# A decoder trunk on one core: the differential mixer's softmax weights transposed by DMA instead of TensorE

## What is computed

```python
def _diff_attention(q1, q2, k1, k2, v, lam):
    ...
        p1 = _masked_softmax(jnp.einsum('bhqd,bhkd->bhqk', q1b, k1).astype(jnp.float32) * scale, mask)
        p2 = _masked_softmax(jnp.einsum('bhqd,bhkd->bhqk', q2b, k2).astype(jnp.float32) * scale, mask)
        p = p1 - lam * p2
        return jnp.einsum('bhqk,bhkd->bhqd', p.astype(v.dtype), v)
```

## Time and profile before

| what | value |
|---|---|
| median of 3 runs | 825.76 us (825.39 to 825.9) |
| profiled execution, its own time | 824.97 us |
| its span, first to last instruction | 823.2 us |
| PE busy | 815.3 us (99%) |
| DVE, ACT, POOL busy | 572.3, 474.9, 291.0 us |
| 16 DMA engines, queue 1 | 68.5% |

### The profile page before, as it was taken

How to read it: one execution, slowest core, us unless ns; L and a number is a source line. 1 busy time by engine, 2 the same in 40 slices (tenths; PEclk the granted TensorE clock), 3 DMA queues, 4 the chain that set the end, 5 groups by cost and what they waited for, 6 DMA issues and landing times.

```text
span 823.2 us, 10986 instructions
## 1 busy us (share of the span) xinstructions
PE 815.3 (99%) x4012; PEld 669.8 (81%) x4012; DVE 572.3 (70%) x837; ACT 474.9 (58%) x709; POOL 291.0 (35%) x301
## 2 busy tenths in 40 slices
PE   9999999999999999999999999999999999999998
PEld 6888878888888888888888888888788888888886
DVE  5696888868765666655456878898697666666542
ACT  6877654794465555443457775557944645545441
POOL 0078874405202433320000789563070043323100
PEclk9999999999999999999999999999999999999999
DMA  9866867784558777775566656767745687777751
GB/s 331 304 149 208 248 180 207 187 252 142 198 185 234 218 208 214 219 221 187 167 203 224 168 205 207 229 192 201 235 154 182 211 215 213 228 227 209 215 185 71
DMA packets 125765, 169.40 MB, mean 206 GB/s; under 512 B 62864, under 2 KB 65168, under 8 KB 125456
## 3 DMA queue, kind: packets, MB, share of 16 engines
q1 hardware_dynamic: 125424, 168.43, 68.5%
q10 hardware_dynamic: 288, 0.27, 0.1%
HBM read 153.47 MB, written 1.05 MB: 188 GB/s over the span
## 4 chain that ended last, share of the span: by engine, by line
PE 90%; POOL 4%; issue 2%; DVE 2%; ACT 1%; DMA 1%; SPq 0%; POOLq 0%; DVEq 0%; ACTq 0%
PE acc L726 83%; POOL p_halves L1549 1%; PE att L869 1%; POOL proj L1482 1%; PE att L805 1%; PE att L773 1%; PE att L860 1%; DMA w_raw<-in_w_in 1%; PE att L798 1%; PE acc L805 1%; POOL proj L1478 0%; DVE za L1327 0%; PE att L843 0%; ACT za L1075 0%; DVE eb L1321 0%
## 5 line engine op out<-in xcount | busy, mean ns | idle before, releaser
L1198 DVE TENSOR_TENSOR w_lo<-w_raw,w_hi 128x1024 fp32r<-128x1024 f32 (+1 forms) x276 | 367.2, 1344 | 147.1 <-ACT w_hi L968 144.6
L726 PE MATMUL acc<-w_hi,xt 128*128 128x512 f32 (+1 forms) x1728 | 431.2, 391 | 0.3 <-ACT xt L991 0.3
L968 ACT ACTIVATE w_hi<-w_raw 128x1024 fp32r<-128x1024 f32 (+1 forms) x275 | 286.2, 1051 | 163.9 <-PE acc L726 153.2
L726 PEld LDWEIGHTS acc<-w_hi,xt 128*128 128x128 f32 x1728 | 319.8, 188 | 65.2 <-issue 1.1
L726 PE MATMUL acc<-w_lo,xt 128*128 128x512 f32 (+1 forms) x864 | 230.0, 388 | 1.6 <-DVE w_lo L1198 1.6
L726 PEld LDWEIGHTS acc<-w_lo,xt 128*128 128x128 f32 x864 | 161.8, 188 | 34.9 <-DVE w_lo L1198 2.2
L1601 POOL COPY hid_t<-hid_halves_t 128x512 uint16<-128x512 uint16 x44 | 35.0, 823 | 95.9 <-DMA hid_halves_t<-hid_halves 81.5
L1592 POOL COPY hid_halves<-hid 128x512 uint16<-128x512 uint16 x44 | 45.6, 1065 | 64.3 <-DVE hid L1277 64.3
L1549 POOL COPY p_halves<-eb 128x768 uint16<-128x768 uint16 x24 | 30.0, 1279 | 97.4 <-DVE eb L1333 60.5
L1462 POOL TENSOR_SCALAR small<-small 128x2 f32<-128x2 f32 (+3 forms) x12 | 9.4, 786 | 152.2 <-ACT sq_dump L1066 133.9
L1609 POOL TENSOR_TENSOR merged<-merged,prod 128x1024 f32<-128x1024 f32 x10 | 32.5, 3254 | 58.0 <-DVE prod L1249 57.1
(11 more groups left out here) (175 smaller groups left out, 715.0 us busy)
## 6 DMA issues: line engine op xcount, KB each, us to landing
w_raw<-in_w_ffn SPq DMA_DIRECT2D x88, 512.0 KB, 4.2
w_raw<-in_w_gate SPq DMA_DIRECT2D x64, 512.0 KB, 4.1
w_raw<-in_w_ffn_down SPq DMA_DIRECT2D x44, 512.0 KB, 4.0
w_raw<-in_w_in SPq DMA_DIRECT2D x39, 512.0 KB, 5.1
w_raw<-in_w_branch SPq DMA_DIRECT2D x16, 512.0 KB, 4.5
w_raw<-in_w_out SPq DMA_DIRECT2D x16, 512.0 KB, 3.3
bg<-in_b_gate SPq DMA_DIRECT2D x8, 512.0 KB, 5.4
w_raw<-in_w_in SPq DMA_DIRECT2D x8, 396.0 KB, 4.3
```

The costliest lines, as they stand in the source:

```text
L726: return pe.matmul(acc[bank0 + t][:, 0:N], x_part[:, k0 + k, t * P:(t + 1) * P], w_part[:, k, 0:N], start=first, stop=last)
L968: act.activation(w_hi[:, n % WR, :, 0:N], w_raw[:, n % RAW, :, 0:N], copy).then_inc(s_hi, 1)
L1198: dve.tensor_tensor(w_lo[:, n % WR, :, 0:N], w_raw[:, n % RAW, :, 0:N], w_hi[:, n % WR, :, 0:N].bitcast(F32), ALU.subtract).then_inc(s_lo, 1)
```

## The change

For B, the eight rows `pt` are taken out of the plan. Heads 0 and 1 are now dealt, transposed and joined together (`pdeal` and `pjoin` of ("B", 0)), heads 2 and 3 as ("B", 1), through one pair of planes of their own, `p_halves_b` and `p_halves_t_b`. Heads 0 and 1 are multiplied with V in turn 30, heads 2 and 3 in turn 38. `o` moves from turn 38 to 39, `deal` D from 31 to 33, `join` D from 35 to 36, SP's transpose for `join` D from its turn 40 to 41. The reduction for `prep` C no longer waits for POOL's `prep` B but for ACT's `brs`, which reads the same small tile. `cks` uses bank `S0` instead of `TP`, and `cs` uses `OB` instead of `S0`.

```diff
-TURNS = [("A", 0), ("A", 1), ("C", 0), ("C", 1), ("D", 0), ("D", 1), ("D", 2), ("D", 3)]
-TURN_P = (21, 22, 43, 47, 52, 53, 55, 56)
-TURN_AT = {33: "C", 40: "D"} | {CHUNKS.index(("ffn", j, 3)) + 9: j for j in range(N_FFN)}
+TURNS = [("A", 0), ("A", 1), ("B", 0), ("B", 1), ("C", 0), ("C", 1), ("D", 0), ("D", 1), ("D", 2), ("D", 3)]
+TURN_P = (21, 22, 32, 40, 43, 47, 52, 53, 55, 56)
+TURN_AT = {33: "C", 41: "D"} | {CHUNKS.index(("ffn", j, 3)) + 9: j for j in range(N_FFN)}
...
-    "Bsm": (22, 22, 30, 30), "Bp": (22, 25, 30, 32), "Bpt": (25, 28, 33, 34), "Bpv": (28, 30, 35, 37), "Bo": 38,
+    "Bsm": (22, 22, 30, 30), "Bp": (22, 25, 30, 32), "Bpdeal": (25, 33), "Bpjoin": (29, 36), "Bpv": (30, 30, 38, 38), "Bo": 39,
...
-    "cpt": 43, "cpv": 51, "Ddeal": 31, "Djoin": 35, "Dsm": (42, 42, 46, 46), "Dp": (42, 42, 46, 47),
+    "cpt": 43, "cpv": 51, "Ddeal": 33, "Djoin": 36, "Dsm": (42, 42, 46, 46), "Dp": (42, 42, 46, 47),
...
-    "Bp": 5.5, "smul": 2, "Apdeal": 0.2,
+    "Bp": 5.5, "smul": 2, "Apdeal": 0.2, "Bpdeal": 0.2, "deal": 5,
...
-    if kind in ("qk", "pt", "kct", "cpt", "cr", "cks", "ck"):
+    if kind in ("qk", "kct", "cpt", "cr", "ck"):
         return (TP,)
     if kind == "sm":
         return (S0, S1)
-    if kind == "cs":
+    if kind == "cks":
         return (S0,)
-    if kind == "o":
+    if kind in ("o", "cs"):
         return (OB,)
...
-    return (first, first + 1), ("pt" if mixer == "B" else "pdeal", (mixer, n))
+    return (first, first + 1), ("pdeal", (mixer, n // 2 if mixer == "B" else n))
...
                 if k > 1:
-                    sp.wait_ge(pjoined.sem, pjoined.at(l, ("pjoin", TURNS[k - 2])))
+                    sp.wait_ge(pjoined.sem, pjoined.at(l, ("pjoin", TURNS[k - 1 if step == ("B", 1) else k - 2])))
...
-                    for s in range(3):
-                        mm = pe.transpose(att[:, TP, s * P:(s + 1) * P], e_map(e)[:, s * P:(s + 1) * P], ident)
...
-                src = ("pt" if mixer == "B" else "pjoin", (mixer, m))
+                src = ("pjoin", (mixer, m // 2 if mixer == "B" else m))
...
-                elif kind == "pt":
-                    act.wait_ge(att_done.sem, att_done.at(l, step))
-                    pb = pt_free(l, step)
-                    act.activation(ptb[:, pb, :], att[:, TP, 0:384], copy).then_inc(read_act.now(step), 1)
...
-                    prev = {"B": ("prep", "D"), "C": ("prep", "B"), "D": ("prep", "C")}[a]
-                    if l or a != "B":
-                        dve.wait_ge(pool_done.sem, pool_done.at(l - (a == "B"), prev))
+                    if a == "C":
+                        dve.wait_ge(act_misc.sem, act_misc.at(l, ("brs", None)))
+                    elif l or a == "D":
+                        dve.wait_ge(pool_done.sem, pool_done.at(l - (a == "B"), ("prep", "D" if a == "B" else "C")))
...
-                                pool.wait_ge(dve_misc.sem, dve_misc.at(l, ("p", a)))
-                            if k > 1:
+                                pool.wait_ge(dve_misc.sem, dve_misc.at(l, ("p", ("B", 2 * a[1] + 1) if a[0] == "B" else a)))
+                            if a == ("B", 1):
+                                pool.wait_ge(s_pturn[(k - 1) % 2], p_turned(l, TURNS[k - 1]))
+                            elif k > 1:
                                 pool.wait_ge(s_pturn[k % 2], p_turned(l, TURNS[k - 2]))
```

More of the change, by code:

```diff
@@ L99 @@
 PAIRS = {"A": 2, "B": 4, "C": 2, "D": 4}
-MAPS = {"A": 0, "B": 4, "C": 0, "D": 0}
 def own_transpose(step):
@@ L158, in steps @@
                 put(PLAN[mixer + kind][n], kind, (mixer, n))
-        for m in range(MAPS[mixer]):
-            for kind in ("pt", "pv"):
-                put(PLAN[mixer + kind][m], kind, (mixer, m))
+        for n in range(2 if mixer == "B" else 0):
+            for kind in ("pdeal", "pjoin"):
+                put(PLAN["B" + kind][n], kind, ("B", n))
+        for m in range(4 if mixer == "B" else 0):
+            put(PLAN["Bpv"][m], "pv", ("B", m))
     put(PLAN["Bo"], "o", "B")
@@ L190, in name_of @@
         return a[0] if a[0] in "oh" or a[1] else a[0] + "0"
-    if kind in ("sm", "p", "pt", "pv", "pdeal", "pjoin"):
+    if kind in ("sm", "p", "pv", "pdeal", "pjoin"):
         return a[0] + kind
@@ L313, in pt_slots @@
     kind, a = step
[L314 to L319, removed]
+    return 2 * (a[1] % 2), 2 * (a[1] % 2) + 1
+PT_USES = [[s for s in keys("pjoin") if s[1][0] != "A" and slot in pt_slots(s)] for slot in range(4)]
 def pv_step(s):
-    return ("pv", s[1])
+    return ("pv", ("B", 2 * s[1][1] + 1) if s[1][0] == "B" else s[1])
 def trunk_kernel(nc, x, x_t, w_in, w_gate, w_branch, w_out, w_ffn, w_ffn_down,
@@ L361, in trunk_kernel @@
                                  for j, at in enumerate(starts) for i in range(2)] for name, starts in turn_at.items())
+        p_halves.append(place("p_halves_b", [P, 2, 2, 384], U16, at=zg_at + 24 * D_MODEL))
+        p_halves_t.append(place("p_halves_t_b", [P, 2, 2, 384], U16, at=zg_at + 8 * D_MODEL))
         xt_raw = place("xt_raw", [P, KT, SEQ], F32, at=zg_at + 16 * D_MODEL)
@@ L529, in p_buffer @@
         def p_buffer(k):
-            return k if k < 2 else 2 + k % 2
+            return k if k < 2 else 4 if TURNS[k][0] == "B" else 2 + k % 2
         def p_turned(l, step):
@@ L830, in scores, with transpose_cp @@
                         score_matmuls(l, maps)
-            def transpose_p(l, step):
+            def transpose_cp(l, step):
                 bank_free(l, step)
[L834 to L841, removed]
-                    for s in range(3):
-                        mm = pe.transpose(att[:, TP, s * P:(s + 1) * P], e_map(e)[:, s * P:(s + 1) * P], ident)
+                pe.wait_ge(dve_misc.sem, dve_misc.at(l, ("cp", None)))
+                for t in range(NT):
+                    mm = pe.transpose(att[:, TP, t * P:(t + 1) * P], cpb[:, t, :, :], ident)
                 mm.then_inc(att_done.now(step), 1)
@@ L855, in times_v @@
                 if mixer == "B":
-                    pb, v0 = pt_slots(src)[0], DFV + m * HD
+                    pb, v0 = m, DFV + m * HD
                     for t in range(NT):
@@ L904, in _ @@
                             scores(l, step)
-                        elif kind in ("pt", "cpt"):
-                            transpose_p(l, step)
+                        elif kind == "cpt":
+                            transpose_cp(l, step)
                         elif kind == "pv":
@@ L920, in _ @@
                             pe.wait_ge(read_act.sem, read_act.at(l, ("ck", None)))
-                            pe.matmul(att[:, TP, 0:HD], cst[:, C_REP:C_REP + P], kpart[:, :], start=True, stop=True
+                            pe.matmul(att[:, S0, 0:HD], cst[:, C_REP:C_REP + P], kpart[:, :], start=True, stop=True
                                       ).then_inc(att_done.now(step), 1)
@@ L934, in _ @@
                                     at = (2 * t + m) * 32
-                                    mm = pe.matmul(att[:, S0, at:at + 32], qkt[1][:, m, t * P:(t + 1) * P],
+                                    mm = pe.matmul(att[:, OB, at:at + 32], qkt[1][:, m, t * P:(t + 1) * P],
                                                    kct[:, :, :].rearrange("p i n -> p (i n)"), start=True, stop=True)
@@ L1140, in do @@
                     for m in range(2):
-                        ins = act.activation(kcs[0:16, m, :], att[0:16, TP, 0:HD], copy)
+                        ins = act.activation(kcs[0:16, m, :], att[0:16, S0, 0:HD], copy)
                     ins.then_inc(read_act.now(step), 1)
```

6 lines of the change are left out of this document (3 added, 3 removed).

## The result

| | before | after |
|---|---|---|
| median | 825.37 us (824.98 to 825.9, 20 runs) | 828.51 us (825.81 to 830.73, 20 runs) |
| ratio | | 1.0037, 95% interval 1.0028 to 1.0045 |
| profiled execution, its span | 824.97, 823.2 us | 825.81, 824.0 us |

The change makes the kernel 3.1 us slower. The forecast was 823.8, and 828.5 lies outside its range of 820.6 to 827.6.

The account below looks back on a forecast made before the run. It took PE, busy 99% of the span, as the bound. D's scores 1.0 us earlier per layer, 2.0 off 824.97, gave 822.97; with 0.79 for the median, 823.8 us, range 820.6 to 827.6.

Parts of the forecast that it names:

- Turn 20: PE's 0.77 us wait for `w_lo`, held behind POOL's `prep` B, goes in each layer.
- Turn 30: Heads 0 and 1: copies 3.6 us, landing 5.1, join ends 97.6; chunk 30 starts at 98.9, 0.4 later.
- The rival that the join holds ACT: First join ends at 98.5, chunk 30 1.3 late, D's scores 1.0 late: 827.8 us; chance 0.16.
- Turns 31 to 38: DVE's C scores at 115.5, `join` C ends 112.4, no PE wait at turn 38, chunk 38 at 124.7, 0.85 earlier.
- Turns 40 and 42: `o` read between 130.2 and 132.0, so `cs` waits none or 1.7 us; `zg` ends between 136.4 and 138.2.
- I take 1.0 earlier, near the good end: D's scores in turn 42 start 1.0 us earlier per layer, from bounds of 1.1 earlier to 0.5 later.
- 0.38 for each of four splits: DVE splits beside POOL's four added copies lengthen by 0.38 us each, 1.5 us a layer by the rows.
- the rule that the prediction weighed: Two-input DVE and SBUF-reading GpSimd instructions lock one port in turns: the four copies cost up to 3.3 us a layer.
- gates hold: DVE keeps its old times, D's scores start within 0.3 of before: 825.8 us (825.2 to 826.4); chance 0.26.
- The start of the sum: The median of the runs stands 0.79 us above the profiled execution's 824.97, so 0.79 is added.
- the stale wait: The reduction at 64.50 stood idle 3.73 us for POOL's `prep` B, costing PE 0.77 a layer; removing it gains that.

Follow-up runs that it names:

- Run 6: Kernel before, only the reduction for C waiting for ACT's `brs` instead of POOL's `prep` B: 823.01 us, ratio 0.9971.
- run 8: Changed kernel, B's DMA transposes on SP cut to 1 of 12 blocks, joins reading a constant: 825.44 us, 825.23 at full clock.
- run 7: Changed kernel, POOL's copies of B cut to 8 columns, transposes and joins reading a constant: 824.56 us, 823.55 at full clock.
- run 11: Changed kernel, copies of B's P made on ACT instead of POOL, everything computed: 822.25 us, ratio 0.9968.
- run 4: Changed kernel, `cs` back in bank S0 and `o` back in turn 38: 826.7 us, ratio 1.0018.
- run 1: Changed kernel once more, no edit: 829.07 us, ratio 1.0038.
- run 3: Changed kernel with five added matmuls that nothing reads, ahead of `cs` alone: 827.06 us, ratio 1.0022.

## Why the prediction was wrong

Point by point, by its own steps, layer 0:

- **Turn 20.** The wait of 0.77 is gone, as said. Run 6 gives it 2.3 us for both layers by the medians (1.3 by the traces), where the sum had 2 x 0.77.
- **Turn 30.** POOL's copies took 3.52 (3.6 forecast) and began 0.5 us earlier than the forecast had them, since turn 25's transpose, off PE's list ahead of them, was left out of their start. The landing was 3.69 and not 5.1, so the join ended at 95.45 and not 97.6, and did not hold PE. It is still in the chain above: DVE stood 0.42 us at 96.58 for the split of chunk 32 behind it. PE waited 1.17 ahead of `ck` (1.7 forecast), and chunk 30 started at 97.58, not 98.9. The rival that the join holds ACT fell with this; it needed an end after 98.3. In run 8, where the landing takes 2.3 us and this wait is gone, DVE ends these two splits no earlier (97.90 for 97.83).
- **Turns 31 to 38.** DVE's C scores began at 115.15 (115.5 forecast), `join` C ended at 110.6 (112.4), chunk 38 started at 124.65 (124.7). But this was partly luck: the forecast has no wait of PE between, and there is one of 1.15 ahead of chunk 36. I followed the four attention banks and not the lent result bank, though C's scores at 115.5 already put its reader behind PE.
- **Turns 40 and 42.** `o` was read until 131.36 and `zg` until 137.64, both inside the bounds (130.2 to 132.0, 136.4 to 138.2).

**The step that failed** is "I take 1.0 earlier, near the good end": D's scores came 0.11 us later in layer 0 and 0.84 later in layer 1. Its reason, that an earlier PE shortens DVE's waits, held (the 0.72 ahead of C's scores is gone), but DVE filled the time with longer instructions. I had worked out what the contention costs beside the first copies alone (0.38 for each of four splits), and credited the stretches that the moved POOL work left. Beside those copies it cost nothing new, since `prep` D had stood there before: the three splits at 86.14 took 4.74 for 4.89. The runs showed that POOL's work does not leave DVE's path, it slides along it: 2.65 us came back at 103.58 and 118.48, and the splits at 109.53, 111.82 and 123.76, with C's second weights and the step at 133.24, lost 5.1. The price of the contention was put at 1.5 us a layer by the rows and at up to 3.3 by the rule that the prediction weighed, and neither figure became a term of the sum. Measured from after at full clock to the copies on ACT it is 826.85 - 822.25 = 4.6 us, 2.3 a layer, between the two. D's scores came out where the rival "gates hold" put them in layer 0 (+0.11) and not in layer 1 (+0.84), and the 826.85 at full clock lies 0.4 above the top of its range of 825.2 to 826.4.

**The rest of the miss** was in no case of the forecast: the clock. Of the 4.7 us between 823.8 and 828.5, 3.0 stand at full clock (826.85), where runs 7 and 11 put them on POOL's copies and run 8 a part on the transposes, and 1.7 are the clock that falls in 14 of 20 executions, behind the wait ahead of `cs` wherever a trace caught it. The forecast had even priced that wait (none, or 1.7 us) without asking what PE's idling does to the clock. The start of the sum hid a little more: it added 0.79 us for the median of three executions of before, and over 20 this is 0.40, so the same steps would have given 823.4.

Open: why the clock falls in some executions and not in others with the same waits, and why a wait of 1.34 us ahead of D's scores (run 4) costs none where one of 1.19 to 1.66 ahead of `cs` does. How much of the copies' price is DVE's longer instructions and how much POOL's later work was not told apart: runs 7 and 11 take both away. By what way the transposes cost 1.6 us is open, and so is what the stale wait's 2.3 us hold beside PE's own 2 x 0.77.

## What to carry to other kernels

Work taken off the busiest engine pays only if what replaces it does not touch the engine that is one step behind. Before crediting it, list what shares a port with the engine that gates, and follow the displaced work to where it comes to lie, not only to where it left. A copy that can go to ACT, which was idle for 4.03 and 6.24 us in the very places and beside whose copies DVE's splits took what they take without them (4.88 for three where before has 4.89, 2.34 for two), was here worth 4.6 us at full clock against the same copy on POOL. And a change of several parts should be split before it is judged: one edit of this one was worth 2.3 us, and the rest hid it.

## What the hardware showed that was not expected

- Behind a wait of PE of 1.25 us the granted clock went from 1.00 to 0.50 for some 3.4 us and cost 1.6 us (run 1); one of 1.19 us was followed by the same, and one of 1.50 us in another execution was not; 14 of 20 executions of the same program have a mean clock of 0.995 to 0.998. With five matmuls that nobody reads ahead of that wait it stayed at 1.00 (run 3).
- POOL copies of 16 elements a partition took 1127 to 2518 ns beside DVE's two-input splits, longer than an undisturbed copy of 768 (819 ns); making a contended copy small hardly shortens it (run 7).
